# The low part of every second up half slab made by GpSimd in the loop of the last feed-forward

## The reference

```
D_FF_2 = 4 * D_MODEL          # 4096

h2 = rms_norm_2(x, norm2_g[l])
x = x + jnp.square(jax.nn.relu(h2 @ w_ff_up[l])) @ w_ff_down[l]
```

## Time and profile before

| | |
|---|---|
| median of the runs | 811.59 us |
| the profiled execution, first to last instruction | 809.6 us |
| TensorE busy | 804.9 us (99%) |
| VectorE busy | 589.1 us (73%) |
| ScalarE busy | 473.8 us (59%) |
| GpSimd busy | 42.6 us (5%) |
| granted TensorE clock over the span | 1.00 |
| read from HBM | 140.37 MB, 175 GB/s over the span |

### The profile page before, as it was taken

How to read it: one execution, slowest core, us unless ns; L and a number is a source line. 1 busy time by engine, 2 the same in 40 slices (tenths; PEclk the granted TensorE clock), 3 DMA queues, 4 the chain that set the end, 5 groups by cost and what they waited for, 6 DMA issues and landing times.

```text
span 809.6 us, 12641 instructions
## 1 busy us (share of the span) xinstructions
PE 804.9 (99%) x4892; PEld 691.3 (85%) x4892; DVE 589.1 (73%) x908; ACT 473.8 (59%) x700; POOL 42.6 (5%) x88
## 2 busy tenths in 40 slices
PE   9999999999999999999999999999999999999998
PEld 8877889888888888888888888999998888888886
DVE  6885799988778788577988863686576855566654
ACT  6876456655656566877565655655844744344442
POOL 0000000000000000003242510100000000000000
PEclk9999999999999999999999999999999999999999
DMA  9953344565555563744454453334355556655551
GB/s 330 351 165 105 105 150 163 188 209 176 192 181 197 197 221 118 275 154 159 160 194 154 169 193 121 105 106 140 128 202 162 185 175 206 208 175 188 172 191 52
DMA packets 90351, 142.08 MB, mean 176 GB/s; under 512 B 3840, under 2 KB 56768, under 8 KB 90176
## 3 DMA queue, kind: packets, MB, share of 16 engines
q1 hardware_dynamic: 89728, 140.38, 51.9%
q10 hardware_dynamic: 576, 1.05, 0.4%
HBM read 140.37 MB, written 1.05 MB: 175 GB/s over the span
## 4 chain that ended last, share of the span: by engine, by line
PE 96%; DVE 2%; DMA 1%; SPq 1%; issue 0%
PE bank L511 21%; PE bank L512 21%; PE bank L513 21%; PE bank L584 16%; PE bank L586 8%; PE bank L382 3%; PE bank L1108 1%; PE bank L1131 1%; DMA vec<-in_vectors 1%; PE bank L1044 1%; DVE w_lo L1782 1%; SPq L413 0%; PE bank L724 0%; PE bank L1068 0%; PE bank L748 0%; PE bank L815 0%
## 5 line engine op out<-in xcount | busy, mean ns | idle before, releaser
L1782 DVE TENSOR_TENSOR w_lo<-raw,w_hi 128x1024 fp32r<-128x1024 f32 (+1 forms) x254 | 302.0, 1215 | 58.4 <-ACT w_hi L1259 57.8
L1259 ACT CAST w_hi<-raw 128x1024 fp32r<-128x1024 f32 (+1 forms) x254 | 260.0, 1045 | 106.7 <-PE bank L513 104.0
L584 PE MATMUL bank<-a_both,w_hi 128*128 128x512 f32 x544 | 193.1, 398 | 0.0
L586 PE MATMUL bank<-a_both,w_lo 128*128 128x256 f32 x544 | 152.7, 281 | 0.0
L511 PE MATMUL bank<-w_hi,h_both 128*128 128x512 f32 (+1 forms) x336 | 133.3, 397 | 0.3 <-DVE w_lo L1782 0.2
L513 PE MATMUL bank<-w_hi,h_both 128*128 128x512 f32 (+1 forms) x336 | 130.4, 388 | 0.0
L512 PE MATMUL bank<-w_lo,h_both 128*128 128x512 f32 (+1 forms) x336 | 130.4, 388 | 0.0
L584 PEld LDWEIGHTS bank<-a_both,w_hi 128*128 128x128 f32 x544 | 102.2, 188 | 25.1
L511 PE MATMUL bank<-w_hi,a_both 128*128 128x512 f32 (+1 forms) x270 | 106.6, 395 | 0.0
L513 PE MATMUL bank<-w_hi,a_both 128*128 128x512 f32 (+1 forms) x270 | 104.9, 389 | 0.0
L512 PE MATMUL bank<-w_lo,a_both 128*128 128x512 f32 (+1 forms) x270 | 104.9, 388 | 0.0
(11 more groups left out here) (234 smaller groups left out, 1038.4 us busy)
## 6 DMA issues: line engine op xcount, KB each, us to landing
raw<-in_w_in SPq DMA_DIRECT2D x45, 1024.0 KB, 5.0
raw<-in_w_up SPq DMA_DIRECT2D x22, 1024.0 KB, 5.0
raw<-in_w_ff_up SPq DMA_DIRECT2D x16, 1024.0 KB, 5.5
raw<-in_w_ff_down SPq DMA_DIRECT2D x16, 1024.0 KB, 4.8
raw<-in_w_down SPq DMA_DIRECT2D x11, 1024.0 KB, 5.0
raw<-in_w_out SPq DMA_DIRECT2D x8, 1024.0 KB, 4.9
raw<-in_w_gla_branch SPq DMA_DIRECT2D x4, 1024.0 KB, 5.0
raw<-in_w_attn_branch SPq DMA_DIRECT2D x2, 1024.0 KB, 4.9
```

What stands on the lines that cost most here:

```text
L584: nc.tensor.matmul(acc.rearrange("p (o t) -> p o t", o=2), w_hi[:, q, k * P:(k + 1) * P], src[:, :, k, :], start=k == 0, stop=False)
L586: ins = nc.tensor.matmul(acc[:, 0:TOKENS], w_lo[:, q, k * P:(k + 1) * P], src[:, 0, k, :], start=False, stop=k == KT - 1)
L1259: nc.scalar.copy(dst, raw_half(m % RAW, half, size, cols)).then_inc(s.hi_done, 1)
L1782: nc.vector.tensor_tensor(dst, raw_half(n // 2 % RAW, n % 2, size, cols), h, ALU.subtract).then_inc(s.lo_done, 1)
```

## The change

GpSimd gets a loop at the end of its program that makes the low part of half b+7 (the second half of an up slab) in each of the 12 loop chunks, once that half's high part is counted, and then counts `second_lo` up. VectorE makes b+6 as before; b+7 is gone from its list. Its two down halves are made by a new function: b+8 without counting `lo_done`, then a wait for `second_lo`, then b+9, which counts `lo_done` up by 3 (for b+7, b+8 and b+9). The first chunk and the last three are as before.

```
+            def up_second_lo(n, i=None):
+                gp.wait_ge(s.hi_done, n + 1 if i is None else i * 12 + n + 1)
+                nc.gpsimd.tensor_tensor(w_lo[:, n % RING, :].rearrange("p (k c) -> p k c", c=P), raw_half(n // 2 % RAW, 1, HALF, 256),
+                                        w_hi[:, n % RING, :].bitcast(F32).rearrange("p (k c) -> p k c", c=P),
+                                        ALU.subtract).then_inc(s.second_lo, 1)
+            n3 = 2 * M_FF2
+            with gp.Fori(0, CH2 // 3 - 1) as i:
+                for e in range(3):
+                    up_second_lo(n3 + 4 * e + 7, i)
...
+            def down_lo(n, i, chunk):
+                dve.wait_ge(s.hi_done, i * 12 + n + 1)
+                nc.vector.tensor_tensor(w_lo[:, n % RING, :], raw_half(n // 2 % RAW, 0, HALF, 0),
+                                        w_hi[:, n % RING, :].bitcast(F32), ALU.subtract)
+                dve.wait_ge(s.hi_done, i * 12 + n + 2)
+                dve.wait_ge(s.second_lo, chunk)
+                nc.vector.tensor_tensor(w_lo[:, (n + 1) % RING, :], raw_half(n // 2 % RAW, 1, HALF, 0),
+                                        w_hi[:, (n + 1) % RING, :].bitcast(F32), ALU.subtract).then_inc(s.lo_done, 3)
...
-                    ff2_chunk(i * 3 + e + 1, (e + 1) % 3, lambda: lo(b + 6, b + 7, i=i), lambda: lo(b + 8, b + 9, i=i))
+                    ff2_chunk(i * 3 + e + 1, (e + 1) % 3, lambda: lo(b + 6, i=i), lambda: down_lo(b + 8, i, i * 3 + e + 1))
```

More of the change, by code:

```diff
@@ L210 @@
     "mix_taken mix_ready mix_hi mix_lo "
-    "up_low up_summed up_square up_hi up_lo last_down"
+    "up_low up_summed up_square up_hi up_lo last_down second_lo"
 ).split()
```

## The result

The changed kernel takes 814.95 us (median of 4 runs, 814.77 to 815.10) where the kernel before takes 811.60; the ratio is 1.0042 with a 95% interval of 1.0028 to 1.0055. It is slower by 3.35 us, beyond the bound of 0.2% and inside the range of 811.4 to 824.5. The profiled execution has a span of 813.1 us, 3.5 more than before.

A forecast was written before the change was run, and what follows sets the result against it. The prediction took TensorE, gapless in this stage, to bound the kernel. Work removed and the moved count were worth 0; a stall of 0.46 us in 12 chunks added 5.5 to 811.6, giving 817.1 us, range 811.4 to 824.5.

The forecast's parts named there:

- what bounds: Last feed-forward loop: TensorE, without gaps, sets the 11.11 us chunk; removing VectorE's 1.22 us pass is worth 0.
- the moved count: b+7's release moves from 655.39 to behind b+9's low part; alone it costs 0, cover shrinking from 3.6 to 0.13 us.
- exclusion in both directions: In the loop, GpSimd's pass and VectorE passes with two SBUF inputs hold each other up; VectorE is held 2.1 us.
- The 4.57 us of the earlier trace: At 409.88, a GpSimd operation of 0.22 us alone took 4.57, beside four VectorE passes; read as VectorE excluding GpSimd.
- the 0.04 us of the earlier trace: At 388.53, a VectorE pass pair took 2.39 us instead of 2.35 with GpSimd let in; read as GpSimd holding VectorE.
- GpSimd's size: GpSimd's added 128x1024 pass: 2.1 ns an element, adding 2.1 us (1.8 to 2.5) beyond the small operation.
- the stall: TensorE's wait at b+7's weight load, in each of 12 chunks: 0.46 us a chunk, 5.5 us in all.
- both orders: GpSimd let in at once or behind the activations' low part: VectorE ends b+9 at 659.46 or 659.45.
- the down load: SyncE issues it later, with the next up load; hidden with 1.2 + 1.5 us cover. Late-load rival: near 823 us, chance 0.03.
- No exclusion: Rival: in the loop GpSimd and VectorE read side by side, b+7 is released at 658.92; 811.6 us, chance 0.16.
- GpSimd let in late: Rival: GpSimd starts behind b+8 or runs slower; 0.75 us a chunk, 820.6 us, or 825.2 at 2.5 ns; chance 0.17.
- The gain: Rival: the changed kernel gets faster, though TensorE waits nowhere in this stage; chance 0.02.

The follow-up runs named there:

- the late count without GpSimd: Against the kernel before: VectorE still makes b+7, but counts it with b+8 and b+9, by 3 behind b+9, with no GpSimd pass; 811.59 us, ratio 1.0001.
- GpSimd second: Changed kernel with GpSimd's pass made to wait also for the activations' low part of the same chunk; 818.57 us, ratio 1.0087.
- pass of 896: Changed kernel with GpSimd's pass cut from 1024 to 896 columns, leaving out low parts of 128 columns of each b+7; 811.95 us, ratio 1.0006.
- 256 columns more: Changed kernel with a second GpSimd operation of 256 columns, to a scratch area, ahead of the count VectorE waits for; 821.63 us, ratio 1.0126.

## Why the prediction came out as it did

**Right: what bounds.** TensorE had no wait to lose, and VectorE's relief was worth nothing. That 1.22 us passes went away shows nowhere in the time.

**Right: the moved count.** Its price alone is zero (the late count without GpSimd: 811.59 us) and the cover that it leaves is as small as forecast, 0.06 us against the 0.13 of the working.

**Right: exclusion in both directions.** The 4.57 us of the earlier trace rows were the strong sign, the 0.04 us of the earlier trace rows a weak one. The trace shows VectorE held for 2.20 us (2.89 for 0.69) of the 2.26 us between the end of b+6's pass and GpSimd's end. The Trainium skill (SBUF — State Buffer, section on the two separate sides) says so as an exclusive lock; here the trace agrees, with the memset as the exception that the page allows for (it counts only GpSimd operations that read SBUF against a VectorE pass with two SBUF inputs).

**Right: GpSimd's size.** 2.1 ns an element from shapes of 8 and 16 gave 0.22 + 2.14 = 2.36 us; unheld it took 2.39 (the run with GpSimd second). The passes with 128 columns less and 256 more give 2.1 ns a column as well.

**Mis-sized: the stall, 0.46 us a chunk by the working and 0.28 by the trace.** Two terms, both too high. The first is the path of VectorE behind GpSimd. I let three passes start afresh at GpSimd's end, 0.03 + 2.96 us. In fact it took 659.60 - 656.79 = 2.81 us by the last pass's end, 0.18 less than my 2.99: the held pass had begun at 654.45 and had only 0.55 us to go when GpSimd ended. GpSimd's own end was 0.05 us later than worked out (2.26 for 2.21 behind b+6's pass). Together b+9 was ready 8.24 us behind the copy, not 8.37. The second term is on TensorE: I took a late weight load at its full price. The runs give the exchange. Lateness is the end of b+9's pass behind the copy, plus 0.05, less 7.96; the cost is a twelfth of the added time:

| kernel | b+9 ready behind the copy | late | cost a chunk |
|---|---|---|---|
| late count, no GpSimd | 659.18 - 651.33 = 7.85 | -0.06 | 0.00 |
| pass of 896 | 659.18 - 651.20 = 7.98 | 0.07 | 0.42 / 12 = 0.04 |
| the changed kernel | 659.60 - 651.36 = 8.24 | 0.33 | 3.35 / 12 = 0.28 |
| GpSimd second | 660.41 - 651.86 = 8.55 | 0.64 | 7.11 / 12 = 0.59 |
| 256 columns more | 660.86 - 652.06 = 8.80 | 0.89 | 10.10 / 12 = 0.84 |

From the changed kernel on, each microsecond late costs a microsecond, less a fixed 0.05 us. So 0.46 - 0.13 - 0.05 = 0.28. Why 0.05 us are free is open: a weight load starts ahead of its matmul (659.05 and 659.16 in the earlier trace rows), so some lateness could be taken from that lead, but no run here tests it.

**Wrong: that both orders end alike.** The working had 659.46 and 659.45. They came out 0.31 us apart, 8.24 us behind the copy when GpSimd goes first and 8.55 when it goes second, because in the second order GpSimd started 0.17 us behind the pass it followed and then took 2.39 us, together 2.56 us where the working had 2.21. The changed kernel took the first order, so its time doesn't show the slip.

**Right for the changed kernel, with less cover: the down load.** SyncE's timeline has the two loads 0.65 us apart, not 0.4:

```profile
659.78 0.37 SPq L393 DMA_DIRECT2D raw<-in_w_ff_down  x1
660.43 0.37 SPq L393 DMA_DIRECT2D raw<-in_w_ff_up  x1
```

The down loads landed in 5.0 us (at most 5.3), this one at about 664.8, and ScalarE took it up at 665.65, so 0.9 us of cover and not 1.2. In the loop no ScalarE wait is put down to a load; the up loads, queued right behind, landed in 7.4 us instead of 5.5, with a chunk in hand. But in three of the other kernels (the late count without GpSimd, 256 columns more, GpSimd second) the down load of one chunk took 6.6 to 6.8 us, and b+8's high part waited for it by 0.58, 0.93 and 0.70 us. ScalarE in the first of them:

```profile
699.34 1.05 ACT L1267 CAST w_hi<-raw 128x1024 fp32r<-128x1024 f32 x1 [0.58 <-DMA raw<-in_w_ff_down]
```

It cost TensorE nothing: those chunks took 11.10, 11.95 and 11.74 us, inside the spread of the others of their kernel. The first 1.2 us of the cover do get used up; the 1.5 us behind it held.

**The rivals.** No exclusion fell to the stretched rows. GpSimd let in late didn't happen in the changed kernel: it got in at the first boundary in all 12 chunks. The gain didn't come. The kernel before has both cases several times: four small GpSimd operations took 4.57 or 4.58 us, and eight took 1.06 to 1.14 us, about one VectorE pass each. Why GpSimd was let in at a boundary in all these chunks and in the earlier trace rows, but not in the burst of the earlier trace rows, no run here settles.

No version here beats the kernel before. The best of those with GpSimd (b+7 counted with b+8) ties with it, as it must while TensorE has no gap in the stage.

## What to carry to other kernels

Ask first whether the engine that carries the chain waits at all; here it didn't, and relief on another engine could only cost. When a signal is bundled with a later one, work out from the timeline how early it still comes: here a cover of 3.6 us shrank to 0.06 us at no price, and a second edit that was harmless by itself then cost 3.35 us. Moving a two-input pass from VectorE to GpSimd wasn't parallel work here, because the VectorE passes beside it have two SBUF inputs: a 1.2 us pass came back as 2.2 us of stall on VectorE, and the stall shows as one long row on it, not as a wait.

## What the hardware showed beside

- A GpSimd subtraction of two 128x1024 float32 inputs takes 2.39 us when nothing holds it; its row has 2.87 us when it has to wait for a VectorE pass to end. Both engines' rows include the time in which an operation is held.
- A memset of 128x1024 on GpSimd takes 0.95 us and runs beside VectorE's two-input passes without stretching them. A copy of the same size holds VectorE by about 0.83 us (1.52 for 0.69).
- Two GpSimd operations queued back to back don't keep VectorE out between them: the pass that waited for the first ran to its end before the second was let in, and the next one was then stretched by 0.55 us.
